# An expert loop on Trainium2: the shared expert as three token-tile steps, four fixed groups, cleared rows under the gates

## What is computed

```python
scores = jax.nn.sigmoid((t @ w_router).astype(jnp.float32))
_, idx = jax.lax.top_k(scores + b_router.astype(jnp.float32), TOP_K)      # 8 of 64
...
routed = jnp.einsum('tef,efd->td', act, w_down_e)
shared = (jax.nn.silu(t @ w_gate_s) * (t @ w_up_s)) @ w_down_s
return (routed + shared).reshape(bsz, l, d)
...
x = x + g2 * moe(h2, ...)
y = rmsnorm(x, final_norm_w)
```

## Time and profile before

| | us |
|---|---|
| median of 3 runs | 1021.3 |
| lowest, highest | 1020.84, 1022.47 |
| the profiled execution, first to last instruction | 1021.6 |
| PE busy | 929.6 (91%) |
| DVE, ACT, POOL busy | 365.8, 185.9, 104.1 |
| data moved | 324.25 MB, mean 317 GB/s |

### The profile page before, as it was taken

How to read it: one execution, slowest core, us unless ns; L and a number is a source line. 1 busy time by engine, 2 the same in 40 slices (tenths; PEclk the granted TensorE clock), 3 DMA queues, 4 the chain that set the end, 5 groups by cost and what they waited for, 6 DMA issues and landing times.

```text
span 1021.6 us, 12985 instructions
## 1 busy us (share of the span) xinstructions
PE 929.6 (91%) x4915; PEld 481.5 (47%) x4915; DVE 365.8 (36%) x711; ACT 185.9 (18%) x277; POOL 104.1 (10%) x205
## 2 busy tenths in 40 slices
PE   4899899999999999999999999997998897988785
PEld 0454456677555568644444444442433343433332
DVE  3309613137200325442344333333232233232256
ACT  2140320112001002202222112221111121211111
POOL 2000000000000000020212122121121121111100
PEclk9999899999999999999999999998999999999998
DMA  9745556522363359798999999999999999999994
GB/s 373 266 165 213 193 212 206 182 65 76 110 237 130 108 181 421 311 395 357 363 373 418 419 420 419 421 420 419 420 419 421 423 420 419 420 421 420 422 419 199
DMA packets 82384, 324.25 MB, mean 317 GB/s; under 512 B 10350, under 2 KB 39194, under 8 KB 52368
## 3 DMA queue, kind: packets, MB, share of 16 engines
q1 hardware_dynamic: 66864, 289.43, 71.0%
q0 software_dynamic: 10080, 24.44, 6.1%
q10 hardware_dynamic: 5376, 9.52, 2.6%
HBM read 301.52 MB, written 34.11 MB: 329 GB/s over the span
## 4 chain that ended last, share of the span: by engine, by line
PE 78%; DVE 8%; DMA 5%; issue 5%; ACT 3%; SPq 1%; DVEq 0%; ACTq 0%
PE bank L522 25%; PE bank L1680 18%; PE bank L551 13%; PE bank L1837 4%; PE bank L1824 4%; DMA arena<-expert_rows 3%; DMA arena<-in_w_mod_dram 2%; PE bank L509 2%; PE bank L1744 2%; PE bank L1864 2%; ACT arena L533 1%; PE bank L540 1%; DVE arena L536 1%; PE bank L1665 1%; PE bank L482 1%
## 5 line engine op out<-in xcount | busy, mean ns | idle before, releaser
L522 PE MATMUL bank<-arena 128*32 128x512 f32 (+2 forms) x1536 | 266.0, 613 | 35.6 <-issue 34.6
L1680 PE MATMUL bank<-arena 128*128 128x384 f32 x640 | 211.8, 492 | 4.7 <-DVE arena L1072 4.7
L522 PEld LDWEIGHTS bank<-arena 128*32 128x32 f32 (+2 forms) x1536 | 94.0, 127 | 204.7 <-issue 203.9
L1680 PEld LDWEIGHTS bank<-arena 128*128 128x128 f32 x640 | 121.8, 192 | 97.0 <-issue 9.9
L551 PE MATMUL bank<-arena 128*32 128x512 f32 (+2 forms) x768 | 131.5, 595 | 6.6 <-issue 5.9
L551 PEld LDWEIGHTS bank<-arena 128*32 128x32 f32 (+2 forms) x768 | 44.7, 123 | 70.2 <-issue 70.2
L564 ACT ACTIVATE arena<-arena 128x1024 f32<-128x1024 f32 x36 | 41.3, 1148 | 166.3 <-DVE arena L560 163.7
L556 DVE SCALAR_TENSOR_TENSOR arena<-bank,arena 128x512 f32<-128x512 f32 x36 | 27.0, 751 | 108.0 <-PE bank L551 107.9
L496 POOL DMA_INDIRECT arena<-h_rows,arena x36 | 38.4, 1067 | 240.4 <-issue 124.3
L536 DVE TENSOR_TENSOR arena<-arena,bank 128x256 f32<-128x256 f32 x36 | 21.8, 606 | 113.5 <-ACT arena L533 113.5
L533 ACT ACTIVATE arena<-bank 128x256 f32<-128x256 f32 x36 | 22.3, 619 | 204.6 <-PE bank L522 204.6
(11 more groups left out here) (246 smaller groups left out, 713.6 us busy)
## 6 DMA issues: line engine op xcount, KB each, us to landing
arena<-in_w_gate_e_dram SPq DMA_DIRECT2D x64, 1024.0 KB
arena<-in_w_up_e_dram SPq DMA_DIRECT2D x64, 1024.0 KB
arena<-in_w_down_e_dram SPq DMA_DIRECT2D x64, 1024.0 KB
arena<-in_w_mod_dram SPq DMA_DIRECT2D x24, 1024.0 KB, 8.2
arena<-in_w_in_dram SPq DMA_DIRECT2D x22, 1024.0 KB, 5.8
expert_rows<-arena SPq DMA_DIRECT2D x6, 2048.0 KB, 23.6
arena<-expert_rows SPq DMA_DIRECT2D x12, 1024.0 KB, 25.3
arena<-mod_rows_out ACTq DMA_DIRECT2D x4, 1024.0 KB, 8.2
```

Source lines behind the costliest of these rows:

```text
L522: ins = pe.matmul(bank[off:off + width, :], x_T[:, k, off:off + width], w[:, :, k, :], start=(k == 0), stop=(k == KT - 1))
L1680: ins = pe.matmul(ps[:, 0:TOK], w[:, k, P * (n % 2):P * (n % 2) + P], hT[:, k, :], start=(k == 0), stop=(k == KT - 1))
```

## The change

Four parts.

1. *The shared expert.* `shared_gate_up`, `shared_down`, their activation and copies are gone. Its weights are a 65th expert (`SHARED`) in a slot of its own; the loop runs over 39 `STEPS`, 36 of rows and three of tokens, behind groups 19, 23 and 27. A token step takes its features from `h2` with no gather, uses all 128 rows, has no look-up, no gate rows and no scatter; `fold_shared` reads the banks of the down projection.
2. *Four fixed groups.* `FIXED` is 4. Group 0 is now fixed expert 0; 1, 2 and 3 are groups 3, 6 and 9. Two of them are loaded right behind `merged_ready`, into slots 4 and 3, the others where 0 and 1 stood, into slots 0 and 1. Slots of later experts are handed out in the order in which they come free. The arena is laid out anew: `g1_rows`, `scale2_rows` and `x1n` lie in slot 2, `shift2_rows` in the last unit of the ring (spread by ScalarE once `mg` is done), `y_conv`, `y_gla` and others in slot 3.
3. *The cleared rows.* The six transfers stand behind the unit loads `gbg` 1 to 3, `wbc` 0, `wbg` 0 and `wbc` 1.
4. *One result buffer.* Rows go to `y_rows`; `weighted_a` of group n waits for the scatter of group n - 1. Only the last group uses `x_g[1]`.

```diff
-FIXED = 2
+FIXED = 4
-BIG, MIDDLE = FIXED + 6, FIXED + 22
+BIG, MIDDLE = FIXED + 4, FIXED + 20
...
-    first = [pairs.pop(0), fixed[0], pairs.pop(0), fixed[1], pairs.pop(0)]
+    first = [fixed[0], pairs.pop(0), pairs.pop(0), fixed[1], pairs.pop(0), pairs.pop(0),
+             fixed[2], pairs.pop(0), pairs.pop(0), fixed[3]]
...
+TILE_AFTER = {19: 0, 23: 1, 27: 2}
+SHARED = NE
...
-    jobs += [("sgu", 0)] + [("hT", NT - 1, i) for i in range(2)] + [("r", NT - 1)]
-    jobs += [("cnt",), ("pos",)]
-    jobs += [("order",), ("sgu", 1), ("sgu", 2), ("ranks",)]
-    jobs += [("shT", t) for t in range(NT)]
-    jobs += [("sy", t, i) for t in range(NT) for i in range(2)]
+    jobs += [("hT", NT - 1, i) for i in range(2)] + [("r", NT - 1)]
+    jobs += [("cnt",), ("pos",), ("order",), ("ranks",)]
...
+        uses = []
+        for i, (kind, n) in enumerate(STEPS):
+            uses += [(i, rank) for rank, off, width in QUADS[n]] if kind == "rows" else [(i, SHARED)]
...
+        slot_of = {0: 4, 1: 3, 2: 0, 3: 1, load_order[FIXED]: 2, load_order[FIXED + 1]: 5}
+        for j, e in enumerate(load_order[NXS:]):
+            old = freed_order[j]
+            slot_of[e], turn_at[e], freed_at[e] = slot_of[old], turn_at[old] + 1, last_use[old]
...
-                    e = pool.value_load(order_i[0:1, rank:rank + 1], min_val=0, max_val=NE - 1)
+                    if rank < FIXED:
+                        e = rank
+                    else:
+                        pool.wait_ge(S["order_ready"], 1)
+                        e = pool.value_load(order_i[0:1, rank:rank + 1], min_val=0, max_val=NE - 1)
...
-                if i == 0:
-                    shared_down()
...
-                if i == 0:
-                    act.wait_ge(S["tile_folded"], 1)
-                    begin_gate(0)
+                if i == 0:
+                    act.wait_ge(S["tokens_ready"], 1)
+                    begin_gate(n)
...
+                for y_in, half, part in (("y_a", 5, slice(0, 512)), ("y_b", 6, slice(512, 1024))):
+                    dve.tensor_tensor(h2[:, t, part], banks[half][:, :], g2_rows[:, SEQ_OF[t], part], ALU.mult)\
+                        .then_inc(x[y_in], 1)
...
-                if i >= 2:
-                    dve.wait_ge(x["scattered"][i % 2], 16 * (i // 2))
-                weighted_a(dve, i % 2, i % 4).then_inc(x["y_a"], 1)
-                weighted_b(dve, i % 2, i % 4).then_inc(x["y_b"], 1)
+                if 1 <= n <= ADDED:
+                    dve.wait_ge(x["scattered"][(n - 1) % 2], 16 * ((n - 1) // 2 + 1))
+                weighted_a(dve, y_of(n), n % 4).then_inc(x["y_a"], 1)
+                weighted_b(dve, y_of(n), n % 4).then_inc(x["y_b"], 1)
...
+                if u in zero_after:
+                    if u == zero_after[0]:
+                        sp.wait_ge(S["no_rows_ready"], 1)
+                    m = zero_after.index(u)
+                    sp.dma_start(all_rows[m // 2][:, 4 * (m % 2):4 * (m % 2) + 4, :],
+                                 no_rows.unsqueeze(1).to_broadcast([P, 4, D])).then_inc(S["rows_zeroed"], 16)
             sp.wait_ge(S["merged_ready"], 1)
-            for n, w in enumerate((w_gate_s, w_up_s)):
-                sp.dma_start(shared_w[:, n, :], w[0].rearrange("(p k) f -> p (k f)", p=P)).then_inc(S["shared_in"], 16)
...
             sp.wait_ge(S["out_done"], 16)
+            for e in range(2):
+                load_gate_up(sp, X[0], e, slot_of[e])
+                load_down(sp, X[0], e, slot_of[e])
...
+            full(act, ("mg", KT - 1))
+            spread(1, shift2_rows).then_inc(S["shift2_in"], 16)
```

381 lines of the change are left out of this document (162 added, 219 removed).

## The result

| | before | after |
|---|---|---|
| median of 4 runs each, us | 1021.88 (1020.84 to 1022.81) | 1026.36 (1025.46 to 1027.29) |
| after / before | | 1.0044, 95% interval 1.0032 to 1.0056 |
| the profiled execution, first to last instruction | 1021.6 | 1024.1 |
| granted TensorE clock, mean | 0.978 | 0.970 |

The change makes the kernel 4.5 us slower; the forecast was 2.2 us faster, and the measured time lies above its whole range. In the two profiled executions the difference is only 2.5 us.

The account below looks back on a forecast made before the run. The prediction took DMA bytes and dry DMA stretches to bound the kernel: first slot 1.7 us earlier plus 0.5 us less dryness, -2.2 us on 1021.6, so 1019.4, or 1019.1 on the median of 1021.3; range 1013.5 to 1024.5.

Parts of the forecast that it names:

- What bounds the kernel: Whole expert loop: bytes moved and dry DMA stretches between the start of the six weight slots and the last read.
- The first slot: Start of the expert loop: first weight slot free at 462.7 us against 464.44, 1.7 us earlier.
- the landing: First group's gather: landed 8 us after its issue, at 451.0 us.
- the 2.6 us that I had taken for the clock: First group's gate and up matmuls: 2.6 us lost to the lower TensorE clock, with ends of 0 and 4.6.
- start no earlier: Rival: late gather or cold clock frees the first slot at 464 to 465 us; time 1020.4 to 1022; chance 0.24.
- The dry queue: DMA after the first freed slot: a 6.4 us hole plus 1.5 of small losses, 7.9 against 8.4, 0.5 us less.
- the ledger: From first freed slot to last read: bytes and dry DMA time of the six weight slots, 0.5 us shorter.
- The rival of held slots: Fixed experts' slots held until steps 3, 6, 9 and the shared expert's slot starve the queue: 1025 us; chance 0.15.
- The clearing is worth nothing: Clearing writes moved under the gates: 30 us won, about as much idle put in its place.
- The token steps are paid from TensorE's waits: Expert loop: three token steps of 13.02 us are covered by 47.6 us of waits; uncovered, the loop is 8 us longer.
- The single result buffer costs nothing: Scatter home 1.3 us before the next `y_done`: no cost. Rival: a slow scatter holds VectorE and TensorE, 1037 us; chance 0.03.
- is as before and moves with the last weights: Tail (reads, sums, norm): unchanged in length, moving with the last weights.

Follow-up runs that it names:

- e16: e7 without the spill code (for tokens beyond a group's block, never run here), token steps moved to behind groups 4, 5 and 7: 1045.14 us, ratio 1.0232.
- e17: e7 without the spill code, token steps moved to behind groups 28, 30 and 32: 1029.70 us, ratio 1.0089.
- e12: The kernel before, without the spill code on all engines: 1021.48 us, ratio 1.0003.
- e13: The kernel before, with two matmuls without use ahead of the first tile's routing matmuls: 1020.59 us, ratio 0.9989.
- e2: The kernel before, with 56 empty semaphore increments at TensorE's start: 1024.89 us, ratio 1.0022.
- e11: The changed kernel timed once more, nothing changed: 1025.87 us, ratio 1.0044 against the kernel before.
- e1: The changed kernel with 64 empty semaphore increments at TensorE's start: 1025.41 us, ratio 1.0028.
- e4: The changed kernel with 33 fillers (matmuls whose result nobody reads) in TensorE's idle time of the routing stage: 1020.21 us, ratio 0.9980.
- e7: e4 with seven more fillers, five before the first group's transposes and two before the first tile's routing matmuls: 1020.47 us, ratio 0.9983.
- e8: e7 with the six clearing writes back behind the last gate, as before the change: 1019.87 us, ratio 0.9983.
- e3: The changed kernel without the spill code (for tokens beyond a group's block, never run here) on all engines: 1025.56 us, ratio 1.0026.
- e15: e7 without the spill code and without the shared expert (three token steps, 3.15 MB): 1012.28 us, ratio 0.9898.
- e14: e10 with e8's placing of the clearing: 1020.62 us, ratio 0.9983.
- e10: e7 with SP asking for the down matrix of group 2's first expert ahead of the second expert's gate matrices: 1019.24 us, ratio 0.9976.

## Why the prediction was wrong, step by step

**"What bounds the kernel" was right.** In every run but e16 and e17, the time from the first free slot to the last read is 542 to 544.5 us (535.7 with 3.15 MB less). The time follows from when the first slot is free and from what the tail adds.

**The first slot: the mechanism was right, one term of its sum was left at nothing.** The gather came at 443.36 (443.0 forecast), the transposes at 451.81 (its landing was put at 451.0), the end of gate and up at 463.4 (462.7). That these times come so near is luck. The third tile's projection, in code that the change leaves alone, ended 1.7 us earlier in this profile than in that of the kernel before, which had lost as much to a fall of the clock at 404 us that e12 and e13 don't have. Counted from the projection's end, the slot came after 45.3 us in three profiles of the kernel before (before, e12, e2), was forecast after 43.5, and came after 45.7 to 45.9 in three of the kernel after (after, e11, e1): 0.5 us later in place of 1.7 earlier.

The step that failed lies ahead of the gather. From the projection's end to its issue it took 25.6 us before, 23.6 were forecast, 25.7 were measured, and with fillers it was 23.2 (e4, e7): 2.1 us are the low clock under the routing steps, for which the sum had no term. Behind the gather the terms held: the landing took 8.45 us for 8.0, and from the transposes to the end of gate and up it was 11.6 for 11.7, with the 2.6 us that I had taken for the clock. In the whole stage the low clock costs 3.8 us (45.8 against 42.0 in e7 and e8), and the fillers of these hold TensorE 1.3 us too long; by the times of e4 and e7 against e3 it is 4.5 (ratios) to 5.4 (medians). With the fall at 404 besides, in e3, the same stage took 47.3 us.

**The rival "start no earlier" described what happened, with too low a price.** It had the cold clock as a cause and ended at 1022, since its 4.6 us were the end of my own range for the term. The rule of the Trainium skill that the prediction cites ("TensorE: Matmul & The Clock Gate", section "Why this matters for your kernels") was borne out, with a granted clock of 0.50 from 425 to 450 us: it was worth more than everything the change gained.

**The dry queue: one hole, as forecast, but longer.** The queue is dry at two places ahead of 500 us and nowhere behind; the losses of 1.5 us later on, which I had added, did not come (419 GB/s from 500 to 540, against 360 for before). Instead, the hole is 8.5 us long for 6.4: 35 us at 332 GB/s are worth 7.3 us of nothing, and 1.2 us lie ahead, because the loads issued at 463.55 had brought 0.1 MB by 465 (49 GB/s from 463 on), and those issued at 476.58 and after brought 176 GB/s from 477 to 479. I had counted the queue as full from the issue on. Against before (0.5 less forecast) the ledger is 0 to 1.1 us longer, 1.0 in this profile. Hardly any of that lies ahead of 540 us (8.5 against 8.4); from 540 to 1000 the queue moved 419 GB/s for 420, which would be 1.1 us. The rival of held slots has the sign, not the mechanism: nothing is dry around steps 3 to 9 or the token steps, but for 411 GB/s in one slice at 800 us.

**The clearing is worth nothing: right** (e8), and its cover under the gates held. **The token steps are paid from TensorE's waits: right** (e15: the bytes alone), and the waits fell from 34.6 to 14.9 us. e16 and e17 show the bounds of that cover, which the forecast had as one number: it exists only between the group at which weights become short and the last few, where TensorE must be early for the final sums. **The single result buffer costs nothing: right.** (Its rival's 1037 us is 16 on the 1021.3 of before; on the forecast it would be 1035.) `weighted_a` (L589) waited for the down projection alone; the row of VectorE's waits in the kernel after:

```profile
DVE arena L589 <- PE bank L584: 110.4, 36, 3.2
```

**The step that failed outright is the sentence that the tail "is as before and moves with the last weights".** The code of the tail is the same; its place among TensorE's instructions is not, and that made it 2.6 us longer in the profile (17.0 for 14.4; 1.8 us by the ratio of e3), with a cause that no term of the sum or rival had.

The sum, by the rows: the first slot 0.5 us later for 1.7 earlier (2.2), the ledger 1.0 longer for 0.5 shorter (1.5), the tail 2.6 longer for nothing (2.6): 6.3 of the 6.7 us between the forecast and the measured difference. The profiles of one kernel differ by as much as the rest (e11 gives 0.3 us less for the tail), and with e3's median in place of the rows the jump would get less and the first slot more, so the shares are less sure than the sum.

**What the change is worth by itself.** With the clock kept up (in e4 up to the gather alone, in its profile) and the jump harmless, e4, e7, e8 and e14 are all 0.17 to 0.20% under the kernel before, about 2 us. That is the forecast's size, but not its sum: it takes matmuls that the forecast kernel doesn't have. But the kernel before also has something to gain from the clock (e13, 0.9989), and against e13 it is under 1 us. The fastest measured is e10, 1019.2 us; that it beats e7 is not established.

## What to carry to other kernels

Work that fills an engine's waits has a second use: before it is moved away, add up every matmul of the stage at the clock that the idle stage will have, from the first gap on, not only the one that is next on the chain. Profile the kernel before more than once where its executions lie apart, and compare like with like: a fall of the clock of a few microseconds in the one profiled execution cost 1.7 us, as much as the forecast had for the first slot. Where a stage begins earlier or later by chance, count its terms from its own start. And a jump over code that never runs is not free: adding or taking instructions far ahead of it can move it to a place where it costs.

## What the runs showed of the hardware

56 empty instructions at the start of TensorE's queue made an otherwise unchanged kernel 3.0 us slower (ratio 1.0022), by a wait of 2.2 us at a jump 950 us later. Instructions come in packets of 16 KB, about one for each 250 of TensorE's instructions, if the queue is TensorE's. How far ahead they are fetched these runs don't show: a jump over some 290 instructions waited at two of the six places that these kernels gave it, by my count.

The granted clock was 0.50 for more than 25 us on end in a stage in which TensorE was busy for 41% (10.25 us of 25), and 0.93 in the same stretch with fillers. In the 1.45 us behind its issue the first load after a dry stretch had brought 0.1 MB, worth 0.2 us at 420 GB/s, so a dry queue cost 1.2 us beyond the wait itself.
